# Expert layer with two large and six small items, a small one first, and three overflow places per expert

## What is computed

```python
logits = (hf @ w_router).astype(jnp.float32) + b_router.astype(jnp.float32)
top_v, top_i = lax.top_k(logits, TOP_K)                 # TOP_K = 2, 8 experts
top_w = jax.nn.softmax(top_v, axis=-1)
combine = jnp.sum(jax.nn.one_hot(top_i, N_EXPERTS) * top_w[..., None], axis=1)
for e in range(N_EXPERTS):
    out = out + combine[:, e:e + 1] * swiglu(hf, w_gate[e], w_up[e], w_down[e])
```

## Time and profile before

| | |
|---|---|
| median of 3 runs | 1556.38 us (1556.24 to 1557.84) |
| the profiled execution's own time | 1555.67 us |
| its span | 1553.9 us |
| TensorE busy | 1498.3 us (96%) |
| VectorE, ScalarE busy | 870.6, 662.7 us |
| DMA traffic | 473.74 MB, mean 305 GB/s |
| expert layer, first product to last landing | about 720 to 1528 us of the span |

### The profile page before, as it was taken

How to read it: one execution, slowest core, us unless ns; L and a number is a source line. 1 busy time by engine, 2 the same in 40 slices (tenths; PEclk the granted TensorE clock), 3 DMA queues, 4 the chain that set the end, 5 groups by cost and what they waited for, 6 DMA issues and landing times.

```text
span 1553.9 us, 18250 instructions
## 1 busy us (share of the span) xinstructions
PE 1498.3 (96%) x7682; PEld 1076.8 (69%) x7682; DVE 870.6 (56%) x873; ACT 662.7 (43%) x660; POOL 13.3 (1%) x18
## 2 busy tenths in 40 slices
PE   8999999999999999999999999989999999999875
PEld 7987887888887987888834783468863688734222
DVE  8458697555458458696730972079941499610103
ACT  4357654433343467654500750057720467400001
POOL 1000000000000000000000000000000000000000
PEclk9999999999999999998999999999999999999998
DMA  9263375555544253369899999999999999999994
GB/s 364 89 243 109 111 253 178 190 189 189 185 169 163 102 224 109 131 233 365 330 421 427 430 430 430 429 431 428 430 387 431 429 429 431 410 431 430 430 429 176
DMA packets 42960, 473.74 MB, mean 305 GB/s; under 512 B 5392, under 2 KB 5520, under 8 KB 7424
## 3 DMA queue, kind: packets, MB, share of 16 engines
q1 hardware_dynamic: 42048, 467.97, 74.6%
q0 software_dynamic: 832, 4.63, 0.8%
HBM read 471.53 MB, written 1.05 MB: 304 GB/s over the span
## 4 chain that ended last, share of the span: by engine, by line
PE 78%; DVE 10%; DMA 6%; ACT 3%; issue 2%; SPq 0%; DVEq 0%; ACTq 0%
PE ps L1797 17%; PE ps L1798 17%; PE ps L1799 17%; PE ps L2213 13%; DMA raw_b<-in_w_item 6%; PE ps L2247 5%; PE ps L2173 2%; DVE lo_a L1153 2%; PE ps L2220 1%; PE ps L1833 1%; ACT w_hi L794 1%; ACT prob_even L902 1%; PE ps L1827 1%; DVE small L1169 1%; ACT w_hi L1048 1%
## 5 line engine op out<-in xcount | busy, mean ns | idle before, releaser
L1153 DVE TENSOR_TENSOR lo_a<-raw_a,w_hi 128x2048 fp32r<-128x2048 f32 (+1 forms) x112 | 246.9, 2212 | 126.2 <-ACT w_hi L794 125.5
L794 ACT ACTIVATE w_hi<-raw_a 128x2048 fp32r<-128x2048 f32 (+1 forms) x112 | 206.3, 1849 | 120.0 <-PE ps L1799 119.2
L1797 PE MATMUL ps<-w_hi,act_hi 128*128 128x512 f32 (+1 forms) x640 | 246.0, 384 | 3.2 <-ACT gates L876 1.3
L1799 PE MATMUL ps<-w_hi,act_lo 128*128 128x512 f32 (+1 forms) x640 | 242.5, 379 | 0.0
L1798 PE MATMUL ps<-lo_a,act_hi 128*128 128x512 f32 (+1 forms) x640 | 242.5, 379 | 0.0
L1529 DVE TENSOR_TENSOR lo_a<-raw_a,w_hi 128x2048 fp32r<-128x2048 f32 x65 | 147.9, 2288 | 24.7 <-ACT w_hi L1048 24.3
L1529 DVE TENSOR_TENSOR lo_b<-raw_b,w_hi 128x2048 fp32r<-128x2048 f32 x58 | 131.8, 2288 | 33.3 <-ACT w_hi L1048 33.1
L1048 ACT ACTIVATE w_hi<-raw_a 128x2048 fp32r<-128x2048 f32 x65 | 124.5, 1918 | 49.9 <-PE ps L1799 48.4
L1797 PE MATMUL ps<-w_hi,x_hi 128*128 128x512 f32 (+1 forms) x352 | 136.5, 388 | 7.3 <-DVE lo_b L1529 6.4
L1797 PEld LDWEIGHTS ps<-w_hi,act_hi 128*128 128x128 f32 x640 | 120.5, 188 | 28.3 <-ACT gates L876 2.3
L1799 PEld LDWEIGHTS ps<-w_hi,act_lo 128*128 128x128 f32 x640 | 120.4, 188 | 23.0
(11 more groups left out here) (266 smaller groups left out, 2151.0 us busy)
## 6 DMA issues: line engine op xcount, KB each, us to landing
raw_b<-in_w_item SPq DMA_DIRECT2D x84, 2048.0 KB, 20.5
raw_a<-in_w_item SPq DMA_DIRECT2D x83, 2048.0 KB, 20.0
raw_a<-in_w_mix SPq DMA_DIRECT2D x60, 1024.0 KB, 5.1
raw_a<-in_w_item SPq DMA_DIRECT2D x44, 1024.0 KB, 5.1
raw_a<-in_w_mix SPq DMA_DIRECT2D x8, 512.0 KB, 3.7
ln_gb<-in_ln_mix POOLq DMA_DIRECT2D x2, 1024.0 KB, 4.8
cst<-in_consts SPq DMA_DIRECT2D x1, 1206.5 KB, 17.0
h<-in_x SPq DMA_DIRECT2D x2, 512.0 KB, 4.2
```

The costliest lines, as they stand in the source:

```text
L794: nc.scalar.activation(w_upper(g)[:, 0:n], raw(slot)[:, 0:n], ACT.Copy).then_inc(s_hi, 1)
L1153: nc.vector.tensor_tensor(w_lo(slot)[:, 0:n], raw(slot)[:, 0:n], w_upper(g)[:, 0:n].bitcast(F32), ALU.subtract).then_inc(s_lo, 1)
L1797: nc.tensor.matmul(dst, xh, wh, start=start, stop=False)
L1799: return nc.tensor.matmul(dst, xl, wh, start=False, stop=stop)
```

## The change

The order becomes one letter per position, all items whole. Position 0 is now the last expert (number 7) and small. Two positions are large, 2 and 5. An expert may have up to three overflow items. Everything that served the halves goes: their extra copy in the weight stream, their unit tables and their split schedules. Since item 0 is small, no unit of it is split ahead, and its tokens are copied as plain fp32 (`copy_tokens(0, False, ...)`), without the lower part.

```diff
-KIND = "BSSBSBSS"
-POS_RANK = [0, 7, 6, 1, 5, 2, 4, 3]
+KIND = "SSBSSBSS"
+POS_RANK = [0, 7, 1, 6, 5, 2, 4, 3]
+FIRST_EXPERT = N_EXP - 1
...
-SEQUENCE = [("F", 0), ("S", 1), ("G", 0), ("S", 2), ("B", 3), ("S", 4), ("B", 5), ("S", 6), ("S", 7)]
+SEQUENCE = [(kind, position) for position, kind in enumerate(KIND)]
...
-OVER, TWICE = 5, 2 * N_EXP
+LEVELS = 3
+OVER, PLACES = 5, LEVELS * N_EXP
...
-    put("tie", np.array([1e6] + [7.0 - e for e in range(1, N_EXP)])[None, :])
+    put("tie", np.array([1e6 if e == FIRST_EXPERT else 7.0 - e for e in range(N_EXP)])[None, :])
...
-            part(0, 0)
+            for k in range(0, ITEM_UNITS, 2):
+                load_pair(ITEM_AT[0] + k, w_item[1 + FIRST_EXPERT, k // 2])
             hold(sp, s_tab, 1)
             for i in range(1, STATIC_ITEMS):
-                kind, col = SEQUENCE[i]
-                if kind == "G":
-                    part(i, ITEM_SIZE["F"])
-                    continue
-                e = sp.value_load(itab[0:1, col:col + 1], min_val=0, max_val=N_EXP - 1)
+                e = sp.value_load(itab[0:1, SEQUENCE[i][1]:SEQUENCE[i][1] + 1], min_val=0, max_val=N_EXP - 1)
...
-                ahead = 1 if l == 0 else 0
-                for k in range(U_UP + 2, U_OUT + 2 + ahead):
+                for k in range(U_UP + 2, U_OUT + 1 if l else U_OUT + 3):
                     split(nb + k + 3, words(k + 3))
...
-            copy_tokens(0, True, FIRST_BANKS)
+            copy_tokens(0, False, FIRST_BANKS)
...
-            gather_matrix(lambda t: rkm[:, t, 0:1], True)
+            gather_matrix(lambda t: rkm[:, t, FIRST_EXPERT:FIRST_EXPERT + 1], False)
             link(nc.vector.tensor_copy(cnt, ps[:, 7, 0:N_EXP]))
...
-            split(MOE_BASE + 1)
             positions()
             numbers()
-            tokens_lo(0, FIRST_BANKS)
-            split(MOE_BASE + 2)
...
-                o5 = [P, 5, OVER, TWICE]
-                each = prod[:, 0:5 * OVER * TWICE].rearrange("p (r a b) -> p r a b", r=5, a=OVER)
-                link(nc.vector.tensor_tensor(each, osel.unsqueeze(1).to_broadcast(o5), over_vals.unsqueeze(2).to_broadcast(o5), ALU.mult))
-                link(nc.vector.tensor_reduce(tab[:, 0:5, N_EXP:POSITIONS], each, AX, ALU.add))
+                for a, b in ((0, 2), (2, 4), (4, 5)):
+                    rows = [P, b - a, OVER, PLACES]
+                    each = prod[:, 0:(b - a) * OVER * PLACES].rearrange("p (r a b) -> p r a b", r=b - a, a=OVER)
+                    link(nc.vector.tensor_tensor(each, osel.unsqueeze(1).to_broadcast(rows), over_vals[:, a:b].unsqueeze(2).to_broadcast(rows), ALU.mult))
+                    link(nc.vector.tensor_reduce(tab[:, a:b, N_EXP:POSITIONS], each, AX, ALU.add))
```

More of the change, by code:

```diff
@@ L135, in constants @@
     put("lower", np.tril(np.ones((N_EXP, N_EXP)), -1).reshape(1, -1))
-    put("tie", np.array([1e6] + [7.0 - e for e in range(1, N_EXP)])[None, :])
+    put("tie", np.array([1e6 if e == FIRST_EXPERT else 7.0 - e for e in range(N_EXP)])[None, :])
     put("posrank", np.array(POS_RANK)[None, :])
-    put("caps", np.array([CAP[k] + CAP["S"] * i for i in range(2) for k in KIND])[None, :])
+    put("caps", np.array([CAP[k] + CAP["S"] * i for i in range(LEVELS) for k in KIND])[None, :])
     put("overj", np.arange(OVER)[None, :])
@@ L180, in item_stream @@
     n = w_gate.shape[0]
-    stream = np.empty((n + 1, ITEM_UNITS, P, 2048), w_gate.dtype)
+    stream = np.empty((n, ITEM_UNITS, P, 2048), w_gate.dtype)
     for f in range(FC):
@@ L189, in item_stream @@
         stream[0, k:k + 2] = part.reshape(2, P, 2048)
[L191 to L209, removed]
+    w0 = 0
+    for g in range(4):
+        width, units = WHOLE.width[g], WHOLE.units[g]
+        for k, w in ((WHOLE.gate[g], w_gate), (WHOLE.up[g], w_up)):
+            part = w[1:, :, w0:w0 + width].reshape(n - 1, units, KT // units, P, width)
+            stream[1:, k:k + units] = part.transpose(0, 1, 3, 2, 4).reshape(n - 1, units, P, 2048)
+        k = WHOLE.down[g]
+        part = w_down[1:, w0:w0 + width, :].reshape(n - 1, units, 2, P, D)
+        stream[1:, k:k + units] = part.transpose(0, 1, 3, 2, 4).reshape(n - 1, units, P, 2048)
+        w0 += width
+    pairs = stream.reshape(n, ITEM_UNITS // 2, 2, P, 2048).transpose(0, 1, 3, 2, 4)
+    return pairs.reshape(n, ITEM_UNITS // 2, P, 4096)
 def slot_of(g):
@@ L974, in mixer @@
                     router_copy(0)
-                for k in range(U_OUT + 5 + ahead, U_OUT + 7):
-                    split(nb + k)
+                if l == 0:
+                    split(nb + U_OUT + 6)
                 root(1)
@@ L1022, in copy_down_hi @@
             def copy_down_hi(it):
-                act.wait_ge(s_used, it.unit(it.size))
+                act.wait_ge(s_used, it.unit(ITEM_UNITS))
                 for half in range(2):
@@ L1068, in hidden_copy @@
                                              ps[:, 6, 0:n // 2 * P], ACT.Copy).then_inc(s_th, 1)
[L1071 to L1072 removed]
+                ahead = [6, 14, 15, 22, 26, 34, 36, 41]
                 splits(split_from, 2)
@@ L1124, in _ @@
             nc.scalar.activation(ee, dd, ACT.Exp).then_inc(s_re, 1)
-            copy_tokens(0, True, FIRST_BANKS)
+            copy_tokens(0, False, FIRST_BANKS)
             nc.scalar.activation(cat[:], h[:], ACT.Copy, scale=ALPHA).then_inc(s_res, 1)
-            item(Item(0), None, 3)
+            item(Item(0))
             for i in range(1, STATIC_ITEMS):
@@ L1414, in mixer @@
                 split(nb + U_OUT + 3)
-                ahead = 1 if l == 0 else 0
-                for k in range(U_OUT + 4, U_OUT + 5 + ahead):
-                    split(nb + k)
+                if l == 0:
+                    split(nb + U_OUT + 4)
+                    split(nb + U_OUT + 5)
                 def summed(t, half):
@@ L2318, in _ @@
             keep_warm(8, 2)
-            gather(0, True, FIRST_BANKS)
+            gather(0, False, FIRST_BANKS)
             item(Item(0))
```

53 lines of the change are left out of this document (20 added, 33 removed).

## The result

| | before | changed |
|---|---|---|
| median | 1556.09 us (6 runs) | 1543.71 us (1540.91 to 1545.86, 6 runs) |
| profiled execution, its span | 1555.67, 1553.9 | 1543.59, 1540.9 |
| TensorE busy | 1498.3 us | 1454.1 us |

The ratio is 0.9936 (95%: 0.9922 to 0.995), 10 us; the medians lie 12.4 us apart. In two more comparisons the changed kernel gave 0.9928 (0.9908 to 0.9948) and 0.9922 (0.99 to 0.9945); over all 19 executions its median is 1542.6 us (1539.4 to 1545.9). The forecast was 1545, the range 1539 to 1551.

What follows compares the result with a forecast made beforehand. The weight stream was taken as the bound, idle 21.4 us; 21.4 - 3.0 (start) - 7.8 (two large items) = 10.6 us less than 1555.67, so 1545 us. Range for 8 in 10: 1539 to 1551.

Steps and rivals of the forecast that it cites:

- A microsecond of idle stream is a microsecond of the total: After 722.6 us, idle weight stream counts fully while TensorE has spare time at the end; 21.4 us idle before the change.
- TensorE's 42 us are worth almost nothing: Third large item made small: 42 us less TensorE work, almost none of it time by itself.
- Start: 15.8 us become 3.0: First item small in place of large: idle stream while it starts falls from 15.8 to 3.0 us.
- TensorE starts at the same time: First item: TensorE begins at about 720.4 us as before, so the first pair is free at 724.0.
- Two dry starts at 3.9 us each: Large items 2 and 5 start on a dry ring: 7.8 us of stalls in place of 3.9 + 1.7.
- The larger table: Three places per expert: VectorE's extra instructions add 2.3 us at most, covered by its 2.46 us wait; 0.
- the splits that went: First item's units 0 to 2 no longer split: 0, at the other end 2.3 us of gain.
- overflow pass: Rival: the loop runs twice for an overflow item, 102.9 us more, time 1648; 4%.
- The clock did not fall in the waits: Rival: TensorE's clock halves in 14 newly waiting pairs, 34 us lost, time 1579; 2%.
- choppy at the start: Rival: refilling one pair at a time keeps the first item's stream slow; 15.8 us stay, time 1558; 3%.
- TensorE wasn't the bound: Rival: TensorE is the bound, so its 42 us less work are gained, time 1514; 1%.
- the end is set by the last byte: Last item: TensorE waits for each next pair, 4.90 us per pair at 430 GB/s, so the stream's last byte sets the end.

Runs made afterwards that it cites:

- changed again: The changed kernel once more, no edit: median 1541.7 us, profiled execution 1544.92 us.
- halves, two large: The kernel before, first large item still in halves, position 5 small in place of large: 1553.3 us, ratio 1.0.
- first large, whole: The kernel before with two large items, the first item large and whole, not in halves: 1559.76 us, ratio 1.005.
- three large: The changed kernel with three large items again (positions 2, 4 and 6), first one small: 1548.81 us, ratio 0.9969.
- later start: The changed kernel with 40 in place of 8 warming matmuls ahead of the first gather: 1546.24 us, ratio 0.9958.
- warming, large items: The changed kernel with 18 warming matmuls at the start of each large item: 1540.19 us, again 1539.38 us.
- three things together: The changed kernel with 18 warming matmuls per large item, 3 for 8 before the first gather, small items' next gather before their last two projections: 1539.26, again 1538.59 us.
- two overflow places: The changed kernel with two overflow places per expert in place of three: 1541.87 us, ratio 0.9927.

## Why the prediction was right, point by point

- *A microsecond of idle stream is a microsecond of the total.* Right, to within 1.7 us in eight profiles. "By the stream" is worked out afterwards from each profile: the profiled time before (1555.67), less what its idle stream is under 21.4 us, plus the shift of the first issue into raw_b against 694.76:

| profile | idle stream | first issue | by the stream | measured |
|---|---|---|---|---|
| changed | 6.1 | 697.39 | 1543.0 | 1543.59 |
| changed again | 9.2 | 696.58 | 1545.3 | 1544.92 |
| halves, two large | 15.2 | 695.27 | 1550.0 | 1551.65 |
| first large, whole | 23.1 | 694.17 | 1556.8 | 1557.29 |
| three large | 14.9 | 695.38 | 1549.8 | 1549.75 |
| later start | 11.6 | 695.62 | 1546.7 | 1546.84 |
| warming, large items | 3.0 | 699.42 | 1541.9 | 1542.18 |
| three things together | 2.5 | 695.96 | 1538.0 | 1538.91 |

  The four other profiles (the changed kernel a third time, two overflow places, and the second ones of the last two kernels) come out within 0.9 us. The last row doesn't count the 1 us that the moved gather takes off the end. The prediction's reason for it, that the end is set by the last byte, was not exact: it is set by a landing about 13 us before it, at the same rate of the stream.

- *TensorE's 42 us are worth almost nothing.* Right: 1.0 (0.9984 to 1.0015) with the third item small and the first one large.
- *Start: 15.8 us become 3.0.* Right in the executions at the low clock (3.1 twice), too much in the one at the full clock (0.1). The step that failed there is "TensorE starts at the same time". At the low clock it holds: 722.20, less the 1.8 us by which that layer began later, is the 720.4 of the prediction. At the full clock the first item began 5 us earlier; the instructions ahead of it are the same, their clock is not.
- *Two dry starts at 3.9 us each.* Both items started dry, at 902.5 and 1213.5; the first was forecast at about 897, some 5 us early, on which nothing hangs, as the ring was dry either way. The stall was 2.9 to 3.3 and 2.8 to 3.1 us; the term was too large by 0.6 to 1.1 each. The small item after them frees pairs in the same way, so why 3.9 came down to 3.0 wasn't settled.
- *Terms taken as 0.* The larger table is 1.3 us longer and lies in a wait of 3.13 us; undone, it changes nothing. What the splits that went are worth was not tried by itself. At the low clock the first item began at the forecast time without them, so no gain of up to 2.3 us shows.
- *The sum.* 10.6 us were forecast, 10 (by the ratio) to 12.4 (by the medians) measured. The profiled pair gives 12.1: 2.9 more at the start and 1.8 more at the stalls than forecast, 2.6 less by the later beginning of the layer, which makes 12.7. That the two first profiles come so near the sum is in part luck, since the full clock at the start and the late layer nearly cancel. Low clock beside low clock the idle stream fell by 12.2 us, 1.6 more than forecast, and this is the stalls' term.
- *Rivals.* No overflow pass (44 transfers of 1 MB). The clock did not fall in the waits of the small items: 43 waits of at most 1.4 us ahead of small products, and 1.00 in each window of 10 us from 720 to 1520 us except where the large items start. There, after 4.9 us of waiting, it was at the low level (0.43 us a matmul), as in the earlier trace rows. The Trainium skill, page "TensorE: Matmul & The Clock Gate", section "HAM oscillation — how this bites in real kernels", describes a loop in which each piece of work is shorter than the wait for the next transfer and each piece starts at the low clock. The trace agrees: with waits of 1.4 us between pieces of 3.65 us it did not fall, and behind each wait of 4.9 us, longer than such a piece, it had fallen. The stream wasn't choppy at the start (429 GB/s), and TensorE wasn't the bound.

## What to carry to other kernels

Where a ring of weights feeds two kinds of work, one slower than the stream and one faster, and the compute engine waits for the stream at the end, count the microseconds in which the stream stands still: they are the time, and the busy share of the compute engine is not. Put the fast kind first, while the ring is full from prefetching, and let the slow kind start on an empty ring, with enough of the fast kind between (with one small item between large ones and after the last, the ring filled and 6.8 us were lost at one place); taking work off the compute engine elsewhere only makes it wait. Before splitting a slow item in halves to soften a full ring, look whether it has to be the first.

## What the runs showed of the hardware that was not expected

The same warming matmuls, in the same place of the same program, ran at the full clock in one execution and at the low one in another: eight took 2.03 or 3.76 us. Of the 13 profiles, the window from 710 to 720 us had a granted clock of 1.00 in 7 and of 0.56 to 0.66 in 6, within one and the same kernel too (1.00 and 0.57). In the changed kernel the first item begins 5 us earlier at the full clock, and the stream loses 0.1 us there in place of 3.1 (4.6 in the low-clock execution with warming matmuls in the large items).

The clock of the rest of the kernel goes with the time as well. An execution's mean granted clock and its time move together: the kernel before took 1559.8 and 1561.4 us in its two executions at 0.985 and 1549.7 to 1552.2 in the eleven at 0.994; the changed kernel took 1545.9 us at 0.985 and 1540.2 at 0.992. The layer's first loads are issued later where the clock was below 1.00 in the mixers, as said above. That the clock is the cause of the whole spread is argued from this and was not tried.
